# A mixture-of-experts stage with a new order in each round, first rows added to the residual table by the DMA itself, and one residual gather a round

## The reference: what is computed

```python
def trunk_layer(x, ...):
    ...
    h = x + mix @ w_out
    y = h + hier_moe(rmsnorm(h, norm_ffn), router_group, router_expert, w_gate, w_up, w_down)
def hier_moe(x, ...):      # 32 experts, each token goes to the best two of one group of eight
    ...
    for e in range(N_EXPERTS):
        hdn = jax.nn.silu(xt @ w_gate[e]) * (xt @ w_up[e])          # 1024 -> 256
        y = y + comb[:, e:e + 1] * (hdn @ w_down[e])                # 256 -> 1024
...
y_prompt = rmsnorm(xp, norm_final)[:, N_META:];  y_sample = rmsnorm(xs, norm_final)
```

## Time and profile before

| | us |
|---|---|
| median of 3 runs | 1003.09 |
| lowest and highest | 993.78, 1004.63 |
| the profiled execution, whole | 998.76 |
| its span | 996.7 |
| around the span | 2.06 |
| mean granted TensorE clock | 0.956 of 2.4 GHz |

### The profile page before, as it was taken

One profiled execution on the slowest core, in us unless ns is written; L12 is line 12 of the kernel. 1 busy time (PEld: TensorE's weight loads), 2 busy tenths in 40 slices (PEclk: granted clock), 3 DMA queues, 4 the chain that ended last, 5 costly groups with the idle time before them and its releaser, 6 DMA issues.

```text
span 996.7 us, 14981 instructions
## 1 busy us (share of the span) xinstructions
PE 894.0 (90%) x5663; PEld 594.7 (60%) x5663; DVE 398.8 (40%) x933; ACT 330.9 (33%) x742; POOL 325.7 (33%) x410
## 2 busy tenths in 40 slices
PE   3899999999999999987799999569999899798991
PEld 3799877888878877766578877333333233232330
DVE  4503533253324523267684435740132523233333
ACT  4523344334443344324442121122231323232331
POOL 1102223233213322111543121021253555464565
PEclk9999999999999999999799999779999899998996
DMA  8132321111121111415245543889999899999942
GB/s 246 46 109 89 106 85 57 64 36 43 44 68 32 34 44 44 138 32 177 82 147 172 174 170 131 354 326 390 376 406 392 344 405 372 398 362 378 352 148 72
DMA packets 89366, 185.52 MB, mean 186 GB/s; under 512 B 21767, under 2 KB 59303, under 8 KB 77006
## 3 DMA queue, kind: packets, MB, share of 16 engines
q1 hardware_dynamic: 69366, 155.55, 42.4%
q0 software_dynamic: 19008, 25.74, 7.6%
q10 hardware_dynamic: 920, 3.27, 1.0%
HBM read 176.17 MB, written 51.85 MB: 229 GB/s over the span
## 4 chain that ended last, share of the span: by engine, by line
PE 59%; DMA 13%; issue 9%; DVE 9%; POOL 6%; ACT 3%; POOLq 0%; SPq 0%; ACTq 0%; DVEq 0%
PE pj L1020 28%; PE pj L1109 10%; DMA hb<-residual,tab 9%; PE pj L1086 4%; PE pj L1071 4%; PE pj L2084 4%; DMA first_rows<-yg,tab 2%; PE tp L1060 2%; DVE hb L2160 2%; PE pj L2126 1%; DMA y<-first_rows,tab 1%; PE pj L1242 1%; POOL y L2018 1%; DVE hb L2146 1%; POOL first_rows L2022 1%
## 5 line engine op out<-in xcount | busy, mean ns | idle before, releaser
L1020 PE MATMUL pj<-n_hi,w_hi 128*128 128x350 f32 (+1 forms) x576 | 198.3, 344 | 3.6 <-DVE n_lo L1340 3.6
L1020 PE MATMUL pj<-n_lo,w_hi 128*128 128x350 f32 (+1 forms) x576 | 188.3, 327 | 0.0
L1020 PE MATMUL pj<-n_hi,w_lo 128*128 128x350 f32 (+1 forms) x576 | 187.5, 326 | 0.0
L2084 PE MATMUL pj<-e_raw,xT 128*32 128x512 f32 (+1 forms) x1280 | 181.8, 614 | 0.0
L1020 PEld LDWEIGHTS pj<-n_hi,w_hi 128*128 128x128 f32 x576 | 109.2, 190 | 35.5 <-issue 33.6
L706 POOL TENSOR_TENSOR w_lo<-w_raw,w_hi 128x1024 fp32r<-128x1024 f32 x21 | 50.7, 2416 | 199.3 <-ACT w_hi L783 199.3
L1020 PEld LDWEIGHTS pj<-n_hi,w_lo 128*128 128x128 f32 x576 | 109.5, 190 | 0.9 <-issue 0.8
L1020 PEld LDWEIGHTS pj<-n_lo,w_hi 128*128 128x128 f32 x576 | 109.6, 190 | 0.6
L1302 DVE CUSTOM_DVE_ANT_0 sc<-pj,strip 128x512 f32<-128x512 f32 (+5 forms) x120 | 60.9, 544 | 119.4 <-PE pj L1086 78.4
L2084 PEld LDWEIGHTS pj<-e_raw,xT 128*32 128x32 f32 (+1 forms) x1280 | 48.6, 118 | 97.8 <-issue 92.6
L2126 PE MATMUL pj<-e_raw,hT 128*32 128x512 f32 (+1 forms) x640 | 87.3, 595 | 0.6 <-ACT hT L2114 0.6
(11 more groups left out here) (288 smaller groups left out, 1340.6 us busy)
## 6 DMA issues: line engine op xcount, KB each, us to landing
e_raw<-in_w_up SPq DMA_DIRECT2D x32, 1024.0 KB
e_raw<-in_w_gate SPq DMA_DIRECT2D x32, 1024.0 KB
e_raw<-in_w_down SPq DMA_DIRECT2D x32, 1024.0 KB
w_raw<-in_w_in SPq DMA_DIRECT2D x24, 512.0 KB, 3.7
first_rows<-logits SPq DMA_DIRECT2D x8, 512.0 KB
wo_raw<-in_w_out SPq DMA_DIRECT2D x8, 512.0 KB, 5.5
k_page<-in_cache_k SPq DMA_DIRECT2D x16, 256.0 KB, 3.2
residual<-h_sb SPq DMA_DIRECT2D x8, 512.0 KB, 4.1
```

Source lines behind the costliest of these rows:

```text
L1020: ins = pe.matmul(pj[g % 2][:, 0:tn], ws[w][:, P * k:P * (k + 1)], x[:, k, t0:t0 + tn], start=(m == 0), stop=(m == 23))
L2084: ins = pe.matmul(gu_bank[r % 2][a:b, :].rearrange("p (q f) -> p q f", q=2), xT[:, r % 2, k, a:b], e_raw[n % RD][:, 0:2, FF * k:FF * (k + ...
```

## The change

The table `y_dram`, its zeros and the ring `y1` go. The DMA adds first rows to `h_dram` in place (an indirect DMA with `compute_op=ALU.add`), so one gather brings residual and first result together, and the DVE add `dve_first` goes. The ring `hb` has six buffers in place of four; the memory of `y1` makes the two new ones. The gather of round n waits until the scatter of round n-2 has landed, as `gather_first` did. The scatters of rounds 22 and 23 are issued only for extra blocks. The order of a round becomes:

- ACT: ht(n-1), square(n-3), silu(n), evac(n-1), xt(n+2).
- DVE: mult(n), out(n-3), z(n-2), the router's piece.
- POOL: gather_x(n+4), scatter_out(n-3), scatter_back(n-1), gather_h(n), root(n-2).

```diff
-        RD, RX, RH, RZ, RO = 5, 3, 2, 2, 4
+        RD, RX, RZ, RO = 5, 3, 2, 6
...
         def gather_h(pool, r):
+            pool.wait_ge(s_back[(r - 2) % RZ], 16 * ((r - 2) // RZ + 1))
...
-        def gather_first(pool, r):
...
+        def add_back(pool, r, idx, src):
+            pool.indirect_dma_start(h_dram, bass.IndirectOffsetOnAxis(ap=idx, axis=0), src, None, bounds_check=TOK - 1,
+                                    oob_is_err=False, compute_op=ALU.add).then_inc(s_back[r % RZ], 16)
...
-            for n in range(NRD + 3):
+            for n in range(-1, NRD):
+                if n + 4 < NRD:
+                    gather_x(pool, n + 4)
                 if DONE0 <= n - 3:
                     scatter_out(pool, n - 3)
-                if n + 3 < NRD:
-                    gather_x(pool, n + 3)
-                if 0 <= n - 2 < NRD:
-                    scatter_back(pool, n - 2)
-                if DONE0 <= n - 1 < NRD:
-                    gather_first(pool, n - 1)
-                    gather_h(pool, n - 1)
-                if DONE0 <= n - 2 < NRD:
-                    pool.wait_ge(s_sq, n - 2 - DONE0 + 1)
-                    root(pool, did, (n - 2) % RO, s_pool)
+                if 0 <= n - 1 < NRD - 2:
+                    scatter_back(pool, n - 1)
+                if DONE0 <= n:
+                    gather_h(pool, n)
+                if DONE0 <= n - 2:
+                    root_of(pool, did, n - 2)
+            scatter_out(pool, NRD - 3)
+            root_of(pool, did, NRD - 2)
+            scatter_out(pool, NRD - 2)
+            root_of(pool, did, NRD - 1)
+            scatter_out(pool, NRD - 1)
...
         def act_m(act):
-            for n in range(-2, NRD + 1):
-                if 0 <= n + 1 < NRD:
-                    act_xt(act, n + 1)
-                if 0 <= n - 1 < NRD:
+            for n in range(-2, NRD):
+                if 0 <= n - 1:
                     act_ht(act, n - 1)
-                if n - 2 >= DONE0:
-                    act_square(act, n - 2)
-                if 0 <= n < NRD:
+                if n - 3 >= DONE0:
+                    act_square(act, n - 3)
+                if 0 <= n:
                     act_silu(act, n)
-                if 0 <= n - 1 < NRD:
+                if 0 <= n - 1:
                     act_evac_dn(act, n - 1)
+                if n + 2 < NRD:
+                    act_xt(act, n + 2)
+            act_ht(act, NRD - 1)
+            act_square(act, NRD - 3)
+            act_square(act, NRD - 2)
+            act_evac_dn(act, NRD - 1)
             act_square(act, NRD - 1)
...
-            for n in range(NRD + 1):
+            for n in range(NRD):
+                dve_mult(dve, n)
+                if DONE0 <= n - 3:
+                    dve_out(dve, n - 3)
                 if DONE0 <= n - 2:
-                    dve_first(dve, n - 2)
                     dve_z(dve, n - 2)
-                if n < NRD:
-                    dve_mult(dve, n)
-                if DONE0 <= n - 2:
-                    dve_out(dve, n - 2)
...
-            dve_first(dve, NRD - 1)
+            dve_z(dve, NRD - 2)
+            dve_out(dve, NRD - 3)
+            dve_out(dve, NRD - 2)
             dve_z(dve, NRD - 1)
             dve_out(dve, NRD - 1)
```

More of the change, by code:

```diff
@@ L192, in step_kernel @@
         idx_cur = keep("idx_cur", [P, 1, 5], I32)
-        fst = keep("fst", [P, 4, 4])
+        fst = keep("fst", [P, 6, 4])
         o_junk = region(512)
@@ L1583, in step_kernel @@
         xg = [at(f"xg{r}", [P, D], F32, r_sc + 4096 * r + 128 * (r // 2)) for r in range(RX)]
-        y1 = [at(f"y1_{r}", [P, D], F32, r0 + 108032 + 4096 * r) for r in range(RH)]
         yg = [at(f"yg{r}", [P, D], F32, o) for r, o in enumerate((r0 + 120320, r_sc + 4096 * 3 + 128))]
-        hb = [at(f"hb{r}", [P, D], F32, o) for r, o in enumerate((r0 + 183296, r0 + 187392, r0 + 191488, r0 + 116224))]
+        hb = [at(f"hb{r}", [P, D], F32, o) for r, o in enumerate((r0 + 183296, r0 + 187392, r0 + 191488, r0 + 108032, r0 + 112128, r0 + 116224))]
         junk16 = at("junk16", [P, D], BF16, r0 + 124416)
@@ L1953, in step_kernel @@
         s_xg = [sem(f"s_xg{i}") for i in range(RX)]
-        s_y1 = [sem(f"s_y1_{i}") for i in range(RH)]
         s_hb = [sem(f"s_hb{i}") for i in range(RO)]
         s_ev = sem("s_ev")
-        s_h1 = sem("s_h1")
         s_xt = sem("s_xt")
@@ L2048, in root, with root_of @@
             pool.tensor_tensor(fst[:, w, 2:3], fst[:, w, 1:2], C("mhalf")[:, 0:1], ALU.pow).then_inc(s_fr, 1)
+        def root_of(pool, did, r):
+            pool.wait_ge(s_sq, r - DONE0 + 1)
+            root(pool, did, r % RO, s_pool)
         y_out, y_smp = O["y_prompt"][0], O["y_sample"].rearrange("b t d -> (b t) d")
@@ L2136, in act_evac_dn, with dve_z @@
                 act.activation(yg[r % RZ][:, 512 * b:512 * (b + 1)], dn[b][:], ACT.Copy, scale=gate_s[:, r:r + 1]).then_inc(s_ev, 1)
-        def dve_first(dve, r):
+        def dve_z(dve, r):
             dve.wait_ge(s_hb[r % RO], 16 * (used(r, RO) + 1))
[L2140 to L2144, removed]
             dve.wait_ge(s_ev, 2 * r + 2)
@@ L2213, in pool_m @@
                 pool.wait_ge(s_hnst[w], 16 * (5 - w))
-            did(pool.memset(y1[0][:, 0:352], 0.0))
-            did(pool.memset(y1[1][:, 376:384], 0.0))
             did(pool.memset(hb[1][:, 24:32], 0.0))
-            did(pool.memset(hb[3][:, 384:512], 0.0))
+            did(pool.memset(hb[3][:, 0:352], 0.0))
+            did(pool.memset(hb[4][:, 376:384], 0.0))
+            did(pool.memset(hb[5][:, 384:512], 0.0))
             pool.wait_ge(s_pool, did.n[0])
@@ L2251, in body @@
                 gather(pool, hb[RO - 1][0:CB, :], h_dram, idx_cur[0:CB, 0, 4:5], s_hb[RO - 1])
-                gather(pool, y1[RH - 1][0:CB, :], y_dram, idx_cur[0:CB, 0, 4:5], s_y1[RH - 1])
                 pool.wait_ge(s_ev, 2 * r + 2)
                 pool.sem_inc(s_turn, 1)
-                scatter(pool, y_dram, TOK, idx_cur[0:CB, 0, 1:2], yg[RZ - 1][0:CB, :], s_back[RZ - 1])
+                add_back(pool, RZ - 1, idx_cur[0:CB, 0, 1:2], yg[RZ - 1][0:CB, :])
                 pool.wait_ge(s_sq, x + (NRD - DONE0 + 1))
@@ L2267, in lists @@
             def lists(pool):
+                for r in (NRD - 2, NRD - 1):
+                    scatter_back(pool, r)
                 pool.wait_ge(s_slots, 4)
```

24 lines of the change are left out of this document (3 added, 21 removed).

## The result

The changed kernel takes 994.11 us (median; 987.89 to 998.22 in 20 runs), the kernel before 1001.28 us (993.78 to 1005.26 in 20 runs). The ratio is 0.993, with a 95% interval from 0.9911 to 0.9948: 7.2 us faster, where 25 us were forecast. The profiled execution took 994.41 us, its span is 992.6 us, the mean granted clock 0.958, so it stands for the median well.

What follows compares the result with a forecast made beforehand. The prediction took PE, with six holes waiting for `hh` from DVE, to set the expert stage's time. 998.76 - 22.9 (holes) - 1.0 (end) + 1.0 (weights) = 975.9 us, say 976; range 966 to 1000.

Steps and rivals of the forecast that it cites:

- Term 1: PE's holes in the expert stage: 16.3 us waiting for `hh` plus 6.6 of slower matmuls, all 22.9 us counted as gained.
- T(n)+14: Round n starts at T(n); its gather, issued about 14 us later behind evac(n-1), has 20 us until it is late.
- the edits at nothing: Zeros, `dve_first`, POOL's gathers, later `act_xt`, new buffers, `gather_h`'s wait: counted as nothing; 0 to 0.5 us gain for the zeros.
- rival (b): Slow adding scatter makes POOL the bound: about 1000 us at L = 20, 1038 at 24; chance 0.15 slower, 0.09 no change.
- rival (c): Another wait in the same place, such as `act_evac_dn` on the scatter, takes over PE's holes: about 1000 us; chance 0.04.
- The formula (L+8)/2: POOL's round, with L from a scatter's issue to its landing; it passes PE's 12.22 us from L = 16.4.
- Term 2: The end after PE's last matmul: 19.0 us against 20.0, so 1 us gained, between -1 and 3.
- Term 3: Weights in the expert stage: loads lag 12 us, 1 us of stall counted; the add takes 0.5 us a round.
- rival (a): The DMA becomes the bound and PE waits for `e_raw`: 10 to 17 us come back, 986 to 993 us; chance 0.10.

Runs made afterwards that it cites:

- run 1: The changed kernel with a plain scatter of first rows that overwrites the residual rows instead of adding: 985.57 us, ratio 0.9868 to the kernel before.
- run 2: Only the new order against the kernel before; table of first rows, its gather and DVE's add kept, rings of two and four: 995.08 us, ratio 0.9937.
- run 5: The changed kernel without the scatter to the sample output, which stays unwritten: 976.69 us, ratio 0.9776 to the kernel before.
- run 6: The changed kernel with each weight load as two DMAs of 4 KB rows instead of one of 8 KB: 989.49 us, ratio 0.9893 to the kernel before.
- run 7: The changed kernel with each weight load as four DMAs of 2 KB rows: 997.82 us, ratio 0.9981 to the kernel before.
- run 9: The changed kernel with only the down weights in 4 KB rows: 986.04 us, ratio 0.9874 to the kernel before.
- run 8: The kernel before the change with weight loads of 2 KB rows: 990.87 us, ratio 0.9908 to the kernel before.
- run 3: Only the DMA's add against the kernel before, in the old order, with one gather and a ring of four: 994.36 us, ratio 0.9936.
- run 4: The changed kernel with the residual gather one POOL round later, four `yg` and four `hb`: 997.34 us, ratio 0.9965 to the kernel before.
- run 11: The changed kernel without the sample scatter and with all weights in 4 KB rows: 982.31 us, ratio 0.9836 to the kernel before.

## Why the prediction was right and wrong

The time lay in the range, 966 to 1000, but the forecast of 976 was 18 us too low, and the gain 7 us where 25 were expected.

**Term 1, what was removed: right.** The six holes on `hh` are gone in all of their places, up to 827 us the rounds are 12.2 us, and the clock was at its upper level over 712 to 778 us (1.00, against 0.96). **Its size: wrong, and this is the step that failed.** The 22.9 us were counted as gained on the ground that the longest transfer in the chain was 16.79 us and that there were 20 us until the gather is late. That carried the delay of the kernel before over to a kernel in which PE doesn't pause, and it left a wait out of the clock: the gather of round n was placed at T(n)+14, behind `scatter_back(n-1)`, though it also waits for the landing of scatter n-2, as `act_evac_dn` of round n does. The prediction names `gather_h`'s wait among the edits at nothing; only rival (b) prices it. It measured 67.9 us for POOL, 59.7 for ACT and, by `hT`, 11.9 of PE's gaps. The gathers themselves landed in 17 to 18 us in the loaded stretch, inside the 20 us; it was the scatter with 23 that was late. The new waits took 18.3 us back. Counted alike in both kernels, from round 9 to round 23 at 12.22 us each and 11.06 for the one without transposes, 24.0 us were lost before and 18.2 after: term 1 gave 5.8 us.

**Rival (b) and rival (c) named the mechanism,** but for another reason and with another course. The formula (L+8)/2 holds: with L = 23 it gives 15.5 us, and POOL's rounds from 779.73 to 888.57 were (888.57-779.73)/7 = 15.5. That its 8 us fit is partly luck. Nothing waited for `out`, so the 3.0 us counted for root and `out` were 0.9; but issuing the two gathers took 1.8 and 2.3 us (864.38 to 869.41) where 1.3 and 1.0 were counted. ACT's evacuation waiting on the scatter of two rounds before was rival (c). Three things were off. L was made to hang on the price of the add; run 1 shows it at 22 without an add. "6 DMAs a round become 5" was taken as relief; but a round also became shorter, from 13.4 to 12.2 us, and POOL's round under load is about 17 us with 6 transfers (run 2), 15.5 with 5 (14.9 plain, run 1) and 12.2 (13.8 at the longest) with 4 (run 5), about 3 us for each. Five don't fit into the 12.2 us of PE, four nearly do: 12.2 is PE's own round, and the landing in run 5 still rose. And the prediction priced L = 20 to 24 over all 19 rounds at 34 to 72 us, less 10 of slack. The landing was at 23 for seven scatters only: the lag took until 827 us to reach PE, and then the holes themselves let the queue recover. The weight queue's share of the engines fell to 39% from 877 to 883 us and to 13% from 898 to 908, and the next scatters (issued at 888.57 and 904.49) landed in 15.7 and 7.7 us instead of 24.2. From 908 to 938 its share was back at 81% and the scatters took 15.7 again, so it wasn't that few weights were left to load. So it cost 18 us and not 62.

**What makes L rise.** Shown: it doesn't hang on the add (run 1), it falls when an almost empty transfer is taken out (run 5), and it falls with weights in shorter rows and smaller transfers at the same number and share of small packets (runs 6, 7, 9), in the old order too with 2 KB rows (run 8). Argued from this: each small packet waits for a weight packet on its engine. The trace has 12349 packets of q0 in 85 transfers, 145 each, or 9 on each of 16 engines; five transfers are 45 an engine, and at 15.5 us a round that is 0.34 us a packet. An estimate from the queues' shares comes out alike: a weight packet took 0.28 us of an engine (74.0% of 250 us on 16 engines for 10487) and a small one 0.07 (21.6% for 12349), 0.35 us for one of each, so 15.8 us for five transfers. The same working gives 18.6 us for the six of run 2 (17 measured), 13.1 for the four of run 5, and 9.7 for the five of run 6, the one of these that stays under PE's 12.2 and whose landing stays short. It would come out the same if an engine alternated between its whole shares of a transfer, 9 packets each, so it doesn't say at what grain the queues take turns.

While PE waits in a hole, its ring of weights is full, the weight queue nearly stands still, and the small packets pass. The kernel before shows it at its first hole: SP waited 18.4 us for PE's down matmuls before it could issue the next load at 785.99, and from 781 to 788 us the queues were

```profile
q0 software_dynamic: 832, 1.00, 45.9%
q1 hardware_dynamic: 44, 0.29, 17.5%
```

In the changed kernel the DMA engines were busy without such a pause from 744 to 852 us (DMA share 1.02). That was the kernel before's relief, and the change removed it along with the holes. The Trainium skill ("DMA: Bandwidth & Descriptors", section "Queues, rings and completion order") says that each DMA engine takes turns between its queues, a whole packet at a time; runs 6 and 7 go the same way, 16.4 us down to 8.6 and 7.6 (medians from 700 to 950) with the weight rows halved and quartered. The trace doesn't show single turns, so the picture stays an inference.

**Term 2, the end: the chain right, a part missed.** The last issue was forecast 15.4 us after PE's end and came at 15.8. The 3.6 us behind it, taken over from before, became 6.5, as POOL's closing drain takes 7.2 us instead of 4.1. So the end is 22.3 us instead of the 19.0 forecast, against 20.0 before.

**Term 3, the price of the add: right.** 0.5 us of the engines a round was taken, 0.5 measured (run 1). The Trainium skill ("Collectives: The Full Stack", section on why ReduceScatter is half of AllGather) says that an add in the DMA costs by its second source read and not by its arithmetic, and the trace agrees by that figure. The stall for weights that was counted (1 us) didn't come in the changed kernel, since the new holes gave the weights their time; where those are cured it comes, 4.1 us in run 5, 5.6 in run 9, 10.1 in run 6. So rival (a) comes next once (b) is cured.

**The sum with what was measured:** 998.76 - 5.8 (term 1) - 0.5 (the stage starts at 660.45 instead of 661.00) + 2.3 (the end) = 994.8, against 994.41.

## What to carry to other kernels

Before crediting a kernel with the removal of PE's pauses, ask what lived on them: here the queue of gathers and scatters caught up while the weight loads stood still, so its delays of before (13 to 17 us for the gathers in the chain, 19 for the scatter) weren't those of after (17 to 18, and 23). Put each new wait on a landing into the clock of the round, also one that never bound before. Count the transfers of a software queue by number, not by bytes, with those that carry almost nothing, and set number times loaded price (3 us here) against the round. Where such a queue is late next to a stream of large rows, splitting a part of the stream into transfers with half the row is a cheap cure up to the point where the stream is missed itself.

## What the hardware showed that was not expected

- How the weight loads are cut sets the delay of the other queue. Rows of 8, 4 and 2 KB (1 MB, 512 and 256 KB a transfer): 16.4, 8.6 and 7.6 us to land (medians from 700 to 950 us). It also costs the engines: 74.0, 77.8 and 83.1% of them for 76 to 77 MB. The rate from 712 to 778 us was 395, 382 and 362 GB/s in the changed kernel, but 403 and 401 in the kernel before with 8 and 2 KB rows.
- An indirect scatter that writes hardly any row still costs packets: without it the same queue moved 16.53 MB in 10761 packets instead of 15.52 MB in 12349, and the kernel was 17 us faster. A skipped row counts as a packet (145 packets a transfer of 128 rows).
- POOL's closing drain isn't constant: 4.1 us in the kernel before and in both of its variants with other weight rows, 4.3 in run 2, 7.0 to 7.2 in the changed kernel and runs 3, 4, 6, 7 and 9, 7.5 in runs 5 and 11, 10.0 in run 1. The four kernels that keep the table of first rows have the short one. In run 1 only the add was removed, so 2.8 us of what that saved on PE's side (10.7 us) were given back there. Each figure is from one profiled execution. What it depends on stays open; it wasn't tried.
